# Chunked scan beside a projection: a segment sum and decay products moved into the middle of a matmul granule

## The reference, cut to what matters

```
cum = cumsum(dt * A)                                  # per head
W[i,j] = (C_i . B_j) * exp(cum_i - cum_j) * dt_j      # j <= i, inside a chunk
y_diag = W @ x
chunk_states = sum_j B_j (exp(cum_end - cum_j) * dt_j) x_j
y_off = (C . h_start) * exp(cum)                      # the decay products
h = exp(cum_end) * h + chunk_states
g = (y + d_skip * x) * silu(z)
g = g * rsqrt(mean(g*g) + eps)                        # per group of 512 channels: "the gate"
mix = concat(ssd_out, conformer_out) @ w_out
```

## Time and profile before

| what | value |
|---|---|
| median of 3 runs | 1800.54 us |
| the profiled execution's own time | 1800.39 us |
| its span in the trace | 1798.8 us |
| TensorE matmul busy | 1779.2 us, 99% of the span |
| VectorE, ScalarE, GpSimd busy | 61%, 43%, 25% |
| granted TensorE clock | 1.00 of full speed in the whole span |
| scan stage | about 545 to 755 us |

### The profile page before, as it was taken

How to read it: one execution, slowest core, us unless ns; L and a number is a source line. 1 busy time by engine, 2 the same in 40 slices (tenths; PEclk the granted TensorE clock), 3 DMA queues, 4 the chain that set the end, 5 groups by cost and what they waited for, 6 DMA issues and landing times.

```text
span 1798.8 us, 34945 instructions
## 1 busy us (share of the span) xinstructions
PE 1779.2 (99%) x13213; PEld 1746.5 (97%) x13213; DVE 1088.6 (61%) x2004; ACT 770.2 (43%) x1139; POOL 453.2 (25%) x352
## 2 busy tenths in 40 slices
PE   8999999999999999999999999999999999999998
PEld 7999999999998898899899999999999999999998
DVE  5577887999788787865875333443434434344444
ACT  6443435555356565633443333333333333333442
POOL 1577776777651122222100000000000000000132
PEclk9999999999999999999999999999999999999999
DMA  8665554555545555564335444444444454444442
GB/s 252 176 189 153 145 157 139 149 152 153 153 144 165 161 177 163 163 215 152 117 123 166 156 140 140 157 156 155 140 140 153 156 158 140 140 151 158 154 143 87
DMA packets 287354, 278.42 MB, mean 155 GB/s; under 512 B 11639, under 2 KB 284767, under 8 KB 286385
## 3 DMA queue, kind: packets, MB, share of 16 engines
q1 hardware_dynamic: 249112, 247.87, 45.4%
q10 hardware_dynamic: 36496, 21.77, 4.1%
q0 software_dynamic: 1648, 7.43, 1.3%
HBM read 261.25 MB, written 17.22 MB: 155 GB/s over the span
## 4 chain that ended last, share of the span: by engine, by line
PE 94%; ACT 2%; DVE 2%; DMA 0%; issue 0%; ACTq 0%; SPq 0%; DVEq 0%
PE ps L1804 28%; PE ps L1806 28%; PE ps L1805 28%; PE ps L1863 1%; PE ps L2087 1%; PE ps L1865 1%; PE ps L1864 1%; PE ps L2060 1%; PE ps L2037 1%; PE ps L2131 1%; PE ps L2132 1%; PE ps L2133 1%; DMA xn<-in_x_prompt 0%; DVE mix L1671 0%; ACT wgt L988 0%
## 5 line engine op out<-in xcount | busy, mean ns | idle before, releaser
L1804 PE MATMUL ps<-ahi,whi 128*128 128x320 f32 x2304 | 717.8, 312 | 0.0
L1806 PE MATMUL ps<-ahi,wlo 128*128 128x320 f32 x2304 | 711.9, 309 | 0.0
L1805 PE MATMUL ps<-alo,whi 128*128 128x320 f32 x2304 | 711.8, 309 | 0.0
L677 ACT ACTIVATE whi<-raw 128x1024 fp32r<-128x1024 f32 (+1 forms) x467 | 479.5, 1048 | 448.6 <-PE ps L1806 382.9
L1205 DVE TENSOR_TENSOR wlo<-raw,whi 128x1024 fp32r<-128x1024 f32 x347 | 424.2, 1245 | 242.4 <-ACT whi L677 239.7
L1804 PEld LDWEIGHTS ps<-ahi,whi 128*128 128x128 f32 x2304 | 432.5, 188 | 1.7
L1805 PEld LDWEIGHTS ps<-alo,whi 128*128 128x128 f32 x2304 | 432.6, 188 | 0.5
L1806 PEld LDWEIGHTS ps<-ahi,wlo 128*128 128x128 f32 x2304 | 432.5, 188 | 0.0
L1804 PE MATMUL ps<-hhi,whi 128*128 128x320 f32 x1016 | 314.3, 309 | 0.0
L1806 PE MATMUL ps<-hhi,wlo 128*128 128x320 f32 x1016 | 313.9, 309 | 0.0
L1805 PE MATMUL ps<-hlo,whi 128*128 128x320 f32 x1016 | 313.9, 309 | 0.0
(11 more groups left out here) (316 smaller groups left out, 1626.3 us busy)
## 6 DMA issues: line engine op xcount, KB each, us to landing
raw<-in_w_in SPq DMA_DIRECT2D x144, 512.0 KB, 3.7
raw<-in_w_up SPq DMA_DIRECT2D x128, 512.0 KB, 4.5
raw<-in_w_down SPq DMA_DIRECT2D x128, 512.0 KB, 4.5
raw<-in_w_out SPq DMA_DIRECT2D x64, 512.0 KB, 3.8
h<-in_state_ssm ACTq DMA_DIRECT2D x16, 512.0 KB, 4.9
out<-hout ACTq DMA_DIRECT2D x16, 512.0 KB, 3.2
x_transposed<-xt ACTq DMA_DIRECT2D x1, 2560.0 KB, 10.1
xr<-x_transposed POOLq DMA_DIRECT2D x1, 2560.0 KB, 9.9
```

Source lines behind the costliest of these rows:

```text
L677: act.activation(whi[:, kq, :, 0:width], raw[:, kq, :, 0:width], ACT.Copy).then_inc(hi_done, 1)
L1804: pe.matmul(out, wh, hi[:, kk, :], start=(kk == 0), stop=False)
L1805: pe.matmul(out, wh, lo[:, kk, :], start=False, stop=False)
L1806: last = pe.matmul(out, wl, hi[:, kk, :], start=False, stop=(kk == NT - 1))
```

## The change

Five things are done together.

1. `segment(T, 1)` and the decay products leave `scan_back` and are issued, as `spans(T)`, in the middle of the second granule: after its first 12 matmuls.
2. On ScalarE the second `decay` stands ahead of the copy of `hts`.
3. The gate's root is split. `gate_keep` copies the mean out of bank 5 where the root stood; the root itself, with its table load, is done at the end of tile j = 1, from SBUF. L2087 of tile j = 1 waits for that copy and no longer for the root. `expect_root` is no longer called there.
4. `stage_x` and `stage_b` are gone: TensorE reads x and B from `xb`.
5. For the last group `gate_keep(3)` and `gate_root(3)` stand where the root stood.

```diff
+            def gate_keep(g):
+                act.wait_ge(gn_mm, g + 1)
+                act.activation(gss[:, g, :], ps[:, 5, 0:TOK], ACT.Copy).then_inc(gn_kept, 1)
+
             def gate_root(g):
-                expect_root()
-                act.wait_ge(gn_mm, g + 1)
-                act.activation(gss[:, g, :], ps[:, 5, 0:TOK], ACT.Sqrt, bias=eps[:, 0:1], scale=float(GROUPS)
+                act.wait_ge(gn_kept, g + 1)
+                act.activation(gss[:, g, :], gss[:, g, :], ACT.Sqrt, bias=eps[:, 0:1], scale=float(GROUPS)
                                ).then_inc(rooted, 1)
...
                     if j == 1 and i >= 1:
-                        gate_root(i - 1)
+                        gate_keep(i - 1)
                     ahead(Q_WC, i, 2 * j + 1)
                     act.wait_ge(ecb_mm, T + 1)
                     if not first:
                         act.wait_ge(y_read, T)
                     act.activation(ecb[:], ps[:, 2, TOK:512], ACT.Copy).then_inc(ecb_ready, 1)
+                    decay(T, 1)
                     act.wait_ge(pstart_done, T + 1)
                     act.activation(hts[:], ps[:, 4, 384:512], ACT.Copy).then_inc(hts_ready, 1)
-                    decay(T, 1)
...
-                    if j == 3 and not final:
-                        stage_b(i + 1)
-                    if not (final and j == 3):
-                        stage_x(T + 1)
+                    if j == 1 and i >= 1:
+                        gate_root(i - 1)
                     store_h(T)
...
-            def granule(pair, kq, bank, hi, lo, tiles=2, by_tile=None):
+            def granule(pair, kq, bank, hi, lo, tiles=2, by_tile=None, between=None):
...
+                    if between and n == 0:
+                        between()
...
-            def scan_back(i, j):
-                T = 4 * i + j
-                first = isinstance(i, int) and i == 0 and j == 0
-                segment(T, 1, first)
-                if not first:
+            def spans(T):
+                segment(T, 1, False)
+                if T:
                     pe.wait_ge(ecb_ready, T)
                 pe.wait_ge(selt_ready, T + 1)
                 pe.wait_ge(mixw_done, 2 * T + 1)
                 pe.matmul(ps[:, 2, TOK:512], selt[:].rearrange("p h d -> p (h d)"),
                           ecum3[:, P:TOK], start=True, stop=True).then_inc(ecb_mm, 1)
 
+            def scan_back(i, j):
...
                 if j == 1 and i:
-                    pe.wait_ge(rooted, 2 + i)
+                    pe.wait_ge(gn_kept, i)
...
-                    granule(Q_WC + 2 * i + p, kq + 1, 0, ahi, alo)
+                    T = 4 * i + j
+                    granule(Q_WC + 2 * i + p, kq + 1, 0, ahi, alo, between=lambda: spans(T))
```

More of the change, by code:

```diff
@@ L152, in build @@
         sc = ar + 5120
-        bt = place("bt", [P, TOK], at=sc)
-        xst = place("xst", [P, TOK], at=sc + 320)
         btok = place("btok", [P, 3, P], at=sc + 640)
@@ L267, in build @@
             sem("var_root"), sem("cn_done"), sem("silu_done"))
[L268 to L271, removed]
+        bt_trans, btok_ready, bm_ready, cb_done = (
+            sem("bt_trans"), sem("btok_ready"), sem("bm_ready"), sem("cb_done"))
+        xtile_trans, xd_ready, seg_done, exp_done, mixw_done = (
+            sem("xtile_trans"), sem("xd_ready"), sem("seg_done"), sem("exp_done"),
             sem("mixw_done"))
@@ L281, in build @@
         gss_done, gn_mm, gn_root, gn_done = sem("gss_done"), sem("gn_mm"), sem("gn_root"), sem("gn_done")
+        gn_kept = sem("gn_kept")
         ghi_done, gact_ready = sem("ghi_done"), sem("gact_ready")
@@ L957, in _ @@
             conf_silu(2)
[L960 to L969, removed]
             def load_h0(T, slot):
@@ L1055, in _ @@
             act.wait_ge(cn_done, 4)
-            stage_b(0)
-            stage_x(0)
             for i in range(3):
@@ L1066, in _ @@
                 ahead(Q_WS, 0, c)
+            gate_keep(3)
             gate_root(3)
@@ L2006, in scan_front @@
                 if j == 0:
-                    pe.wait_ge(bt_ready, i + 1)
                     if not first:
@@ L2015, in scan_front @@
                     for c, off in enumerate((0, P, TOK - P)):
-                        last = pe.transpose(ps[:, 4, c * P:(c + 1) * P], bt[:, off:off + P], ident[:])
+                        last = pe.transpose(ps[:, 4, c * P:(c + 1) * P], xb[:, NT + i, off:off + P], ident[:])
                     last.then_inc(bt_trans, 1)
@@ L2020, in scan_front @@
                         hi = min((c + 1) * P, TOK)
-                        last = pe.matmul(ps[:, 2, c * P:hi], bt[:, off:off + P], xb[:, NT + GROUPS + i, c * P:hi],
+                        last = pe.matmul(ps[:, 2, c * P:hi], xb[:, NT + i, off:off + P], xb[:, NT + GROUPS + i, c * P:hi],
                                          start=True, stop=True)
@@ L2026, in scan_front @@
                     pe.wait_ge(pst_done, T)
-                pe.wait_ge(xst_ready, T + 1)
                 for c, off in enumerate((0, P, TOK - P)):
-                    last = pe.transpose(ps[:, 4, c * P:(c + 1) * P], xst[:, off:off + P], ident[:])
+                    last = pe.transpose(ps[:, 4, c * P:(c + 1) * P], xb[:, T, off:off + P], ident[:])
                 last.then_inc(xtile_trans, 1)
@@ L2073, in scan_back @@
                           ecum3[:, P:TOK], start=True, stop=True).then_inc(ecb_mm, 1)
+            def scan_back(i, j):
+                T = 4 * i + j
+                first = isinstance(i, int) and i == 0 and j == 0
                 pe.wait_ge(xd_ready, T + 1)
```

## The result

The changed kernel takes 1805.99 us, the median of 8 runs (1805.20 to 1806.16), against 1800.51 us for the kernel before (8 runs beside it). The ratio is 1.0029, 95% interval 1.0018 to 1.0040: slower by 5.5 us. The prediction said 1805.4 us, 1801.8 to 1808.2, slower with a chance of 0.73. The profiled execution took 1805.90 us, its span 1804.3, 5.5 more than before.

What follows compares the result with a forecast made beforehand. TensorE, in flight 99% of the span, bounds the kernel, with 4.9 us of scan waits to win. Terms -2.5 + 1.8 + 2.6 + 1.6 + 1.4 + 0.1 = +5.0 on 1800.39 give 1805.4 us, range 1801.8 to 1808.2.

Steps and rivals of the forecast that it cites:

- Tiles 5, 9 and 13, the gain: Wait at `within` goes: table loads leave the tile's middle, second decay starts half a granule earlier, ahead of `hts`; -2.5 us.
- Tiles 6, 10 and 14, the Exp table: Exp table load moves into the first decay, so the decay products come 0.6 us late in each tile; +1.8 us.
- Tiles 7, 11 and 15, the copy of `selt`: GpSimd's copy, held up until VectorE's `gate_mult` ends, makes the earlier decay products wait 0.88 us per tile; +2.6 us.
- Tiles 8 and 12, `hts` behind the decay: ScalarE has no gap there, so `hts` behind the second decay comes 0.8 us late for L2090, twice; +1.6 us.
- One more entry into a granule per tile: TensorE returns once more from decay products to big matmuls, 0.10 us each time, for 14 tiles; +1.4 us.
- Tiles 0 and 1: Scan start: ScalarE 0.88 us ahead and VectorE follows, old waits spared, but new ones in the granule; +0.1 us.
- the margin of 0.35 us: Tile 3: spare time between the first head's weighting and copy of `selt` and the earlier decay products; no wait expected.
- At nothing: Items put at no cost: `xst` and `bt` copies elsewhere, L2087's wait for the copy, the last root, DMAs.
- the copy of `selt` stayed behind `gate_mult`: Rival for tiles 7, 11 and 15: GpSimd's copy comes before `gate_mult`, in time; 1802.8 us, chance 0.11.
- ScalarE was late in both places: Rival: the load in the first decay and the order of `hts` are hidden, 1.8 + 1.6 go; 1802.0 us, chance 0.09.
- a switch did not cost more than its row: Rival: a table switch costs twice its 1.28 us row, adding 3.8 us in three tiles; 1809.2 us, chance 0.04.
- faster: Rival: decay products' four waits end within 2.0 us of the second granule's start in every tile; 1795.5 us, chance 0.06.

Runs made afterwards that it cites:

- the first experiment: The changed kernel with the copy of `hts` ahead of the second decay again, as before the change: 1805.48 us.
- the last version: The changed kernel with `selt` copied early, Exp loaded behind the root, `hts` before the decay in tiles 8 and 12, stores behind the next weight piece: 1798.19 us.

## Why the prediction was right

The time came out 0.6 us above the forecast, and the mechanisms that carried it are those that were seen. The steps, one by one:

- *Tiles 5, 9 and 13, the gain.* Right: 2.77 us against 2.5; the sum took the table of waits, and the tiles were longer by a little more than it shows. Of the three reasons that it gave, only the first counted: the root's move alone gives all of it, without an earlier second decay and with `hts` ahead of it.
- *Tiles 6, 10 and 14, the Exp table.* Right in place and cause, shown by the load behind the root. 0.76 us each against 0.6. The exponential ended 2.08 us behind the granule's start, forecast 2.10; the rest is the hand-over from VectorE to TensorE, 0.15 us (634.56 to 634.71), which the sum left out, and 0.05 more at the weighting.
- *Tiles 7, 11 and 15, the copy of `selt`.* Right, shown by the early copy. 0.99 each against 0.88, again a hand-over (0.09); the copy itself took 1.43 us, 1.41 before.
- *Tiles 8 and 12, `hts` behind the decay.* Right, shown by the order alone. 0.95 each against 0.8: the sum let `hts` be wanted 0.10 us later for the entry, which cost nothing.
- *One more entry into a granule per tile.* Mis-sized, the weakest term: +1.4 forecast for 14 tiles, 0.01 per tile measured. The long first step is there, but the matmuls on either side of the cut became cheaper by as much. The step took the price of one instruction pair and not the length of the whole tile.
- *Tiles 0 and 1.* +0.31 against +0.1. The lead of ScalarE did reach VectorE, but it was 0.7 us and not 0.88: the weighting of the second head in tile 0 ended at 559.21 in place of 559.91, and the first one in tile 1 at 569.62, forecast 569.45. Of the 0.72 from the two copies 0.54 was left at the copy `btok` (550.18 against 550.72). The sum also counted only 0.16 us for the order of `hts`; the first experiment shows that without this order the two tiles cost 2.6 us more.
- *Tile 3.* Left out. The prediction took the margin of 0.35 us as fixed, though the trace of before held a store whose issue took twice its usual time just ahead of it, and a `wlo` that took 1.54 us in place of 1.23 beside GpSimd's squares.
- *The total.* It came near in part by luck. The entries were to cost 1.4 us and cost next to nothing; tile 3, which was left out, cost 0.86, the waits forecast in eight tiles 1.1 more than they were put at, and tiles 0 and 1 0.2 more, against 0.3 more of gain.
- *The range of the main case.* Its terms give 1802.8 to 1807.3 us (1805.4 less 1.4 and eight times 0.15; plus 0.7 and as much), not 1803.2 to 1807.6 as it stands. The measured time lies in both.
- *At nothing.* The last root in the next stage and the wait of L2087 cost nothing, as said.

Of the rivals none came: the copy of `selt` stayed behind `gate_mult`, ScalarE was late in both places, a switch did not cost more than its row, and the decay products found all their waits over in seven tiles only (2, 4, 5, 8, 9, 12 and 13), where "faster" needed all sixteen.

## What to carry to other kernels

On an engine that never rests, moving an instruction forward gains nothing by itself and moves the deadline of everything it waits for; list those waits tile by tile, with the spare time of each, before moving it. Where a change has several parts, try each alone: here one part held nearly the whole gain (2.8 of 3.2 us, the copies' removal the rest), and the two that were put around it cost 8.6 us together. Costs of steps that share an engine's order don't add up: early sums and decay first cost 8.1 and 9.6 us each alone, 8.6 together.

## What the runs showed of the hardware that was not expected

- The issue of a small store from ScalarE's queue took 0.42 us in most tiles, but 0.86 to 2.00 us at one place, 588 to 592 us, in the profiled execution of every kernel here, and again near 665 and 717 us in most. In the profile of the last version these were 1.84, 1.30 and 1.60 us. What makes it slow is open: no experiment here changed the store itself. The one experiment on it took the stores off the path, and the runs' scatter fell from 2.0 to 1.0 us. The versions with early sums scatter by 1.0 to 2.0 us and the two that moved the root alone by 0.4 and 0.7, but that the issue is the reason is not shown: the kernel before, where nothing waits for it, scatters by 0.5 to 1.2 in 15 to 28 runs. Whether it also makes the two runs of the changed kernel at 1805.2 us, against 1805.9 to 1806.2 for the others, was not seen in a profile.
- A GpSimd copy of 0.29 us took 1.43 us when it began inside a VectorE instruction with both inputs in SBUF, and ended 0.16 us behind it. It works the other way round as well: in tile 3 VectorE's `wlo`, two inputs in SBUF, took 1.75 us in place of 1.23 when it began inside a GpSimd instruction.
- A short bf16 matmul of 192 columns in front of the large ones costs 0.03 us, and 0.08 in front of an fp32 one of 128.
